# Rounded pairs for the experts' down product: 19 pieces of its weights prepared in the input projection, 45 in the output projection

## The reference

```
proj = x @ w_in                       # 1024 -> 1536: u, v, xs
y_a  = gelu(u) * spatial_gate(layer_norm(gelu(v)))          # 4 heads, 128x128 causal
y_b  = s5_state_space(xs)             # 32 groups, 64 complex states, then a GLU
x    = layer_norm(ALPHA * x + concat(y_a, y_b) @ w_out)
# grouped top-2 of 16 experts, D_FF = 256
h    = silu(x @ w_gate[e]) * (x @ w_up[e])
out += comb[:, e] * (h @ w_down[e])   # w_down[e]: 256 x 1024
x    = layer_norm(ALPHA * x + out)
```

## Time and profile before

| | |
|---|---|
| median of 3 runs | 1351.86 us (1350.22 to 1351.9) |
| the profiled execution | 1347.4 us, span 1345.8 us from first to last instruction |
| busy share of the span | PE 90%, DVE 66%, POOL 35%, ACT 34% |
| DMA | 222.87 MB, 166 GB/s over the span |
| mean granted TensorE clock | 0.957 of 2.4 GHz |

### The profile page before, as it was taken

One profiled execution on the slowest core, in us unless ns is written; L12 is line 12 of the kernel. 1 busy time (PEld: TensorE's weight loads), 2 busy tenths in 40 slices (PEclk: granted clock), 3 DMA queues, 4 the chain that ended last, 5 costly groups with the idle time before them and its releaser, 6 DMA issues. The chain is left out here.

```text
span 1345.8 us, 22978 instructions
## 1 busy us (share of the span) xinstructions
PE 1209.0 (90%) x6813; PEld 969.9 (72%) x6814; DVE 892.6 (66%) x1980; ACT 462.7 (34%) x696; POOL 475.1 (35%) x552
## 2 busy tenths in 40 slices
PE   7999999799978878999999689999999999999910
PEld 6997999778867745888888576777677677677600
DVE  3452776458877655466667677777777777777585
ACT  4120110100003343222221235555565565555433
POOL 3107850210010004322221144454455455445267
PEclk9999999899989998999999699999999999999965
DMA  8555352564154232433332557787887777645484
GB/s 247 184 204 157 102 173 57 137 247 188 64 144 149 90 132 70 156 110 107 127 107 112 207 184 232 211 261 210 241 226 213 214 214 206 141 94 103 117 313 171
DMA packets 112877, 222.87 MB, mean 166 GB/s; under 512 B 51305, under 2 KB 68281, under 8 KB 103569
## 3 DMA queue, kind: packets, MB, share of 16 engines
q1 hardware_dynamic: 96368, 164.86, 36.4%
q0 software_dynamic: 15408, 55.12, 17.6%
q10 hardware_dynamic: 1040, 2.10, 0.4%
HBM read 144.34 MB, written 77.58 MB: 165 GB/s over the span
## 5 line engine op out<-in xcount | busy, mean ns | idle before, releaser
L2055 DVE TENSOR_TENSOR wgu<-w_raw,wgu (+1 forms) x192 | 226.1, 1220 | 52.5 <-ACT wgu L2142 52.4
L2249 PE MATMUL p_gu<-wgu,xg_high 128*128 x768 | 251.4, 408 | 4.5 <-DVE xg_low L2048 4.5
L2142 ACT CAST wgu<-w_raw (+1 forms) x192 | 187.1, 1050 | 18.9 <-SPq L1863 16.3
L2249 PEld LDWEIGHTS p_gu<-wgu,xg_high 128*128 128x128 f32 x768 | 143.2, 188 | 58.0 <-issue 30.9
L2272 PE MATMUL p_d<-wd,ht 128*128 x384 | 174.9, 598 | 1.8 <-DVE ht L2069 1.0
L2249 PE MATMUL p_gu<-wgu,xg_low 128*128 x384 | 150.3, 391 | 0.0
L2272 PEld LDWEIGHTS p_d<-wd,ht 128*128 128x128 f32 x384 | 69.0, 189 | 71.3 <-issue 71.2
L1721 PE MATMUL p_out<-w_out_high,mixt_high 128*128 128x512 f32 x256 | 101.4, 396 | 0.0
L1721 PE MATMUL p_out<-w_out_high,mixt_low 128*128 128x512 f32 x256 | 99.9, 390 | 0.0
L1721 PE MATMUL p_out<-w_out_low,mixt_high 128*128 128x512 f32 x256 | 99.7, 389 | 0.0
L1934 POOL TENSOR_TENSOR spare_e<-nothing 128x1 f32<-128x1 f32 x48 | 9.2, 192 | 227.7 <-DVE yo L2075 227.7
(11 more groups left out here) (441 smaller groups left out, 2727.2 us busy)
## 6 DMA issues: line engine op xcount, KB each, us to landing
w_raw<-in_w_gate SPq DMA_DIRECT2D x16, 1024.0 KB, 4.7
w_raw<-in_w_up SPq DMA_DIRECT2D x16, 1024.0 KB, 7.7
wd<-in_w_down SPq DMA_DIRECT2D x16, 1024.0 KB, 4.8
acc_rows<-ax SPq DMA_DIRECT2D x18, 512.0 KB, 5.6
xin<-in_x_prompt SPq DMA_DIRECT2D x16, 512.0 KB, 6.2
sq<-sq_mats SPq DMA_DIRECT2D x16, 512.0 KB
z<-in_x_prompt SPq DMA_DIRECT2D x16, 512.0 KB, 4.1
x_rows<-x SPq DMA_DIRECT2D x16, 512.0 KB, 4.8
```

The lines of the kernel that those rows point to most:

```text
L2055: low = tt(wgu[:, slot, 1, at], raw[:, slot, at], wgu[:, slot, 0, at].bitcast(F32), ALU.subtract)
L2142: nc.scalar.copy(wgu[:, slot, 0, at], raw[:, slot, at]).then_inc(hi_set, 1)
L2249: mm = t.matmul(pg[b][:, :, :], x[:, b, k, :], w[h][:, k], start=(k == 0 and x is xh and h == 0), stop=(k == KD - 1 and x is xl))
```

## The change

The down product becomes a product of rounded pairs too. The high and low halves of `w_down` are made once for each expert, ahead of the expert stage, written to DRAM (`wd_dram`) and read back there. The weights are cut into 64 pieces of 128 partitions x 512 columns (2 KB runs), four to an expert. A piece takes one load (SP), one rounding copy (ACT), one subtraction (DVE) and two stores (SP).

- 19 pieces in the input projection, steps 6 to 23 and 26, at most one in a step: load at step n, ACT at n + 1, DVE at n + 2, stores at n + 3. Their room is that of `ya` tiles not yet written (y4 to y7) and of two of the four `xin` slots (x2, x3); x rows go through the other two slots from row tile 4 on, and their loads move behind the stores of odd steps.
- 45 pieces in the output projection, in steps p = 2 to 15: 2, 1, 3, 2, 3, 4, 3, 4, 4, 4, 4, 4, 4, 3. They lie in tiles of `ya` (the piece, then its low half) and `yb` (the high half) that are used up. SP, ACT and DVE have these steps unrolled.
- `ya` and `yb` are laid out by tile of 128 tokens ([P, 16, 4, 128] in place of [P, 4, 2048]).
- Expert stage: two arrays of down weights are loaded in place of one; `ht` gets a high half (ACT) and a low half (DVE); ACT and DVE take the quarters of the weights in another order, with a semaphore for each quarter; the two transposes of the hidden rows stand in the middle of `gate_up`; the rows of ln2 are loaded at the end of the stage.

```diff
@@ input projection
+            SLOTS = {"x2": 30, "x3": 30, "y4": 16, "y5": 20, "y6": 24, "y7": 28}
+            LIFE = 4
+            for n in range(6, 27):
+                free = [s for s in SLOTS if busy.get(s, 0) <= n and n + LIFE <= SLOTS[s]]
+                free.sort(key=lambda s: SLOTS[s])
+                for s in free[:1]:
+                    if len(UNITS) < 19:
+                        UNITS.append((n, s))
+                        busy[s] = n + LIFE
...
+                def rows_in(c):
+                    before = c - 4 if c < 6 else c - 2
+                    sp.wait_ge(turned[before % 4], before // 4 + 1)
+                    sp.dma_start(xin[:, c % 2, :], x_rows[c * P:(c + 1) * P, :]).then_inc(load_x[c % 2], 16)
+
+                def units(n):
+                    for j, s, m in units_at(n - 3):
+                        sp.wait_ge(wd_low, j + 1)
+                        for h in range(2):
+                            sp.dma_start(wd_dram[h][j // 4, :, j % 4 * SUP:(j % 4 + 1) * SUP],
+                                         wd_part(s, 1 - h, True).bitcast(F32)).then_inc(wd_st[s], 16)
+                    for j, s, m in units_at(n):
+                        if m:
+                            sp.wait_ge(wd_st[s], m * 32)
+                        elif s[0] == "x":
+                            sp.wait_ge(turned[int(s[1])], 1)
+                        sp.dma_start(wd_part(s, 0, False), wd_src[j // 4, :, j % 4]).then_inc(wd_ld[s], 16)
...
+                        if i and f % 2 and 2 * i + 4 + f // 2 < CH:
+                            rows_in(2 * i + 4 + f // 2)
+                        units(n)
@@ ACT, u_tile(i, f)
+                    for j, s, m in units_at(i * FT + f - 1):
+                        act.wait_ge(wd_ld[s], m * 16 + 16)
+                        nc.scalar.copy(wd_part(s, 1, True), wd_part(s, 0, False)).then_inc(wd_high, 1)
@@ DVE, xs_tile(i, f)
+                    for j, s, m in units_at(i * FT + f - 2):
+                        dve.wait_ge(wd_high, j + 1)
+                        v.tensor_tensor(wd_part(s, 0, True), wd_part(s, 0, False), wd_part(s, 1, True).bitcast(F32),
+                                        ALU.subtract).then_inc(wd_low, 1)
@@ output projection, SP
+                def units_in(p):
+                    sp.wait_ge(mix_low, p * 2 + 2)
+                    if landed(p - 2, 2, 32):
+                        sp.wait_ge(wd_st[p % 2], landed(p - 2, 2, 32))
+                    for u, t in STEPS_D[p]:
+                        sp.dma_start(ya_u[:, t], wd_src[u // 4, :, u % 4]).then_inc(wd_ld[p % 2], 16)
+
+                def units_out(p):
+                    sp.wait_ge(wd_low, landed(p, 1, 1))
+                    for u, t in STEPS_D[p]:
+                        for h in range(2):
+                            sp.dma_start(wd_dram[h][u // 4, :, u % 4 * SUP:(u % 4 + 1) * SUP],
+                                         (yb_r, ya_r)[h][:, t].bitcast(F32)).then_inc(wd_st[p % 2], 16)
+
+                for p in range(2, CH + 1):
+                    sp.wait_ge(x1_set, p + 1)
+                    if p in STEPS_D:
+                        units_in(p)
+                    if p < CH - 1:
+                        rows_in(p, p % 2)
                     stores(p, p % 2)
+                    if p - 1 in STEPS_D:
+                        units_out(p - 1)
@@ output projection, ACT
+                def units(p):
+                    act.wait_ge(wd_ld[p % 2], landed(p, 2, 16))
+                    for u, t in STEPS_D[p]:
+                        nc.scalar.copy(yb_r[:, t], ya_u[:, t]).then_inc(wd_high, 1)
+
+                for p in range(2, CH):
+                    if p + 2 <= CH:
+                        high(p + 2, p % 2)
                     tile(p, p % 2, p // 2)
                     score(p - 1)
+                    units(p)
@@ output projection, DVE
+                def units(p):
+                    dve.wait_ge(wd_high, landed(p, 1, 1))
+                    for u, t in STEPS_D[p]:
+                        v.tensor_tensor(ya_r[:, t], ya_u[:, t], yb_r[:, t].bitcast(F32), ALU.subtract).then_inc(wd_low, 1)
...
                         norm(i * 2 + b, b, False, i)
                         turn(i * 2 + b - 1, (b + 1) % 2)
+                        units(i * 2 + b - 1)
                     select(i * 2 - 4, 2, i * 2 - 1)
...
                 turn(CH - 1, 1)
+                units(CH - 1)
                 norm(CH, 0, False, CH // 2)
@@ experts, SP
                 def down(e):
-                    sp.dma_start(wd[:, 1 - e % 2, :], a["w_down"][0, expert(e)].rearrange("(p k) f -> p (k f)", p=P)).then_inc(wd_in[e % 2], 16)
+                    for h in range(2):
+                        sp.dma_start(wd[h][:, 1 - e % 2, :].bitcast(F32), wd_dram[h][expert(e)]).then_inc(wd_in[e % 2], 16)
@@ experts, DVE, step
                 def tail(i, b, first):
-                    dve.wait_ge(h_turned, i + 1)
-                    v.tensor_copy(ht[:, b], pt_h[:, :, :]).then_inc(ht_set, 1)
+                    dve.wait_ge(ht_high, i + 1)
+                    tt(ht[1][:, b], pt_h[:, :, :], ht[0][:, b].bitcast(F32), ALU.subtract).then_inc(ht_set, 1)
...
+                        prep(i, slot, range(1))
                     if begun:
                         result(i - 2, b, begun == 1)
                     if not last:
-                        prep(i, slot, range(3))
+                        prep(i, slot, range(1, 3))
                     if begun or b:
                         tail(i - 1, 1 - b, False)
+                    if not last:
+                        prep(i, slot, range(3, 4))
                     hidden(i, b, not begun)
                     if not last:
                         turn(i + 1, 1 - b)
-                        prep(i, slot, range(3, 4))
@@ experts, ACT, step
                     if not last:
                         slot, ready = regs(i)
+                        prep(i, not begun and b == 0, slot, ready)
                     if begun:
                         result(i - 2, b, begun == 1)
                     if not last:
-                        prep(i, not begun and b == 0, slot, ready)
+                        for c in range(1, 3):
+                            quarter(i, slot, c)
+                    if begun or b:
+                        hidden_high(i - 1, 1 - b, not begun or begun == 1 and b == 0)
+                    if not last:
+                        quarter(i, slot, 3)
@@ experts, PE
-                    w = wd[:, slot, :].rearrange("p (k n) -> p k n", k=2)
+                    w = [wd[h][:, slot, :].rearrange("p (k n) -> p k n", k=2) for h in range(2)]
                     for m in range(2):
                         for k in range(2):
-                            mm = t.matmul(pd[m][:, :], ht[:, b, k, :], w[:, k, m * SUP:(m + 1) * SUP], start=(k == 0), stop=(k == 1))
+                            for x, h in PARTS:
+                                mm = t.matmul(pd[m][:, :], ht[x][:, b, k, :], w[h][:, k, m * SUP:(m + 1) * SUP],
+                                              start=(k == 0 and x + h == 0), stop=(k == 1 and x == 1))
...
                     for k in range(KD):
+                        if k == KD // 2 and between:
+                            between()
```

More of the change, by code:

```diff
@@ L136, in hybrid_step @@
         x1_dram = dram("x1_rows", [SEQ + NS, D])
+        wd_dram = [dram(f"w_down_{n}", [E, P, 4 * SUP]) for n in ("high", "low")]
+        wd_src = a["w_down"][0].rearrange("e (p k) (h f) -> e p (k h) f", p=P, h=2)
+        NUNITS = 4 * E
         acc_dram = dram("acc_rows", [SEQ + NS + 2 * P, D])
@@ L396, in _ @@
                 act.wait_ge(w_v_in, 16)
+                for s in ("x2", "x3"):
+                    act.wait_ge(wd_st[s], uses(s) * 32)
                 for k in range(KD):
@@ L1432, in hybrid_step, with landed @@
             x1_stored = [phase_sem(f"x1_stored{i}") for i in range(2)]
+            wd_ld, wd_st = ([phase_sem(f"d_wd_{k}{i}") for i in range(2)] for k in ("in", "stored"))
+            wd_high, wd_low = sems("d_wd_high d_wd_low")
+            STEPS_D, used, left = {}, {}, NUNITS - AUNITS
+            for p in range(2, CH):
+                free = [t for t in range(p) if used.get(t, 0) <= p - 2][:min(3 + (p in (7, 9, 10, 11, 12, 13, 14)), left)]
+                STEPS_D[p] = [(NUNITS - left + k, t) for k, t in enumerate(free)]
+                left -= len(free)
+                used.update((t, p) for t in free)
+            assert left == 0, left
+            def landed(p, of, each):
+                return sum(len(u) for q, u in STEPS_D.items() if q <= p and (q - p) % of == 0) * each
             ax1_stored = [phase_sem(f"ax1_stored{i}") for i in range(2)]
@@ L1691, in _ @@
                     turn(1 + b, 1 - b, b == 0)
+                units(2)
                 dve.wait_ge(sel_set, 7)
                 dve.wait_ge(rb_in, 16)
-                with dve.Fori(2, CH // 2 - 1) as i:
-                    ch.enter(i - 2, 8 + 32)
+                for i in range(2, CH // 2 - 1):
```

(15 more changed lines are left out.)

114 lines of the change are left out of this document (70 added, 44 removed).

## The result

The changed kernel took 1359.26 us (median of 6 runs, 1356.13 to 1361.83) against 1351.19 us of the kernel before on the same chip: ratio 1.0062, 95% interval [1.0044, 1.008]. It is slower by 0.6%. The forecast was 1329 us and "faster" with 0.90, so both sign and time failed.

A forecast was written before the change was run, and what follows sets the result against it. The expert stage was taken to go at PE's pace. Down product -35.5, last tile +0.5, expert DMA +2, output projection +4 and +4.3, input projection +2 gave -22.7: 1351.9 to 1329 us, range 1317 to 1346.

The forecast's parts named there:

- Preparing the pieces, output projection: Output projection: making 45 pieces in 14 steps costs +4 us in the steps and +4.3 at the stage's end.
- SP and DMA term: Output projection: loads queued behind landing stores need 13.8 us against a 13.6 us step; +4 us, bounds 0 and 25.
- Both signs that the prediction named for being wrong: Whole kernel: PE's total does not fall by 35 us, or the two projections together grow by over 20.
- rival C: Output projection: all 14 steps go at the pace of stores landed, then loads; slower, 1373 us, threshold 1352; chance 0.07.
- The end of the stage, +4.3: Output projection's end: the last step's pieces stand before the last norm with nothing covering them; +4.3 us, bounds 2 and 6.
- ACT's and DVE's work: Output projection: copies and subtractions mostly fit DVE's slack; 0 to 1 us a pair of four-piece steps, 4 such pairs.
- Input projection, +2, bounds 0 and 11.6: Input projection: 19 pieces, one a step, mostly covered, ACT 1 to 2 us late in places; +2 us, bounds 0 and 11.6.
- The down product, -35.5: Expert stage: 12 rounded products at p_gu's 0.228 us save 0.74 us a tile over 48 tiles, -35.5 us.
- DMA in the experts, +2: Expert stage: 14 more loads of 1.05 MB fit by 3% but land later; +2 us, bounds 0 and 15.
- Rival A: Expert stage: it slips off PE as gate_up waits for xg_low; +14 us at 0.3 us a tile, 1343 us; chance 0.12.
- B: Expert stage: the DMA engines fill up, with 92% busy in two-tile experts; 1344 us; chance 0.10.
- D (1321): Both projections: preparation is hidden but for the output projection's tail; -30.7 us, 1321 us; chance 0.16.

The follow-up runs named there:

- run 11: Changed kernel with the output projection's piece loads and stores left out, ACT's and DVE's work kept on a resident row, unrounded down weights read: 1333.34 us.
- run 9: Changed kernel with 40 output-projection pieces, the last step's behind the last norm, tiles reused after three steps, unrounded down weights read: 1339.5 us.
- run 10: Same kernel as run 9, but tiles reused after two steps, so SP waits for the stores of step p - 2: 1348.09 us.
- run 7: Changed kernel with three output-projection orders changed and high halves not stored, experts reading them from w_down itself: 1334.99 us, ratio 0.9888 to the kernel before.
- run 2: Changed kernel storing only 128 of 512 columns of each output-projection half, experts reading unrounded down weights: 1343.99 us.
- run 5: Changed kernel with only the last step's three pieces moved behind the last norm, on ACT and DVE: 1352.03 us.
- run 4: Changed kernel with no pieces prepared in either projection, experts reading unrounded down weights: 1321.64 us, ratio 0.98 to the kernel before.
- run 8: Changed kernel with one step more between a piece's load and ACT's rounding in the input projection, steps 4 to 24: 1346.38 us.
- run 3: Changed kernel without the 45 output-projection pieces, the 19 input-projection pieces kept, experts reading unrounded down weights: 1326.33 us.
- run 1: Changed kernel with ACT rounding the output projection's pieces one step later: 1356.61 us, ratio 1.0056 to the kernel before.
- run 12: Changed kernel with the order of run 5, the single store of run 7 and the lead of run 8: 1331.83 us, ratio 0.9856 to the kernel before.

## Why the prediction was wrong

**The step that failed** is "Preparing the pieces, output projection", its SP and DMA term: +4, bounds 0 and 25. With the transfers that also struck the end of the stage, it measured 25.8 us (run 11 against the kernel after: 18.0 in the loop, 7.8 at the end). The mechanism was named, and its pair of numbers was "even", 13.8 against 13.6; I then took a value near the lower bound. Both signs that the prediction named for being wrong came: the two projections grew by 38.5 us together, and PE's busy time fell by 15.1 us and not by 35 (27 less in the experts, 11 more in the output projection, 2 more in the input projection). Three errors lay in the 13.8:

- *The rate.* 400 GB/s was read in two microseconds. It does occur in this traffic (417 and 397, above), but only for 4 us behind the loads; over 50 us it is 341 at full share, and 4.72 MB take 13.8 us and not 11.8. That alone is PE's step of 13.6. The Trainium skill, "DMA: Bandwidth & Descriptors", section Where 436 GB/s comes from, gives about 358 GB/s for a core's HBM side. Over a step the trace stays below it; inside a step it was exceeded again (417), so the page's figure is no ceiling here, but as a mean it would have served better than mine.
- *The turn.* I allowed 2 us of latency between the last store's bytes and the next load's. It measured 17.2 - 13.8 = 3.4 us a step (the share of 0.80). Behind it stands SP: it needs 8.0 us to issue 4 loads, z, x, the accumulator and 6 stores (661.62 to 669.6), and 8.7 to 11.2 with 8 stores, a cost that was in no term, and only then can the last landing begin to be waited for (8.2 us). Making that wait one step older gave 6 us (runs 9 and 10); one store fewer, which cuts issue, bytes and wait at once, gave 12 (run 7).
- *"Only six steps have four."* By the forecast's own list seven have four, and steps 7 to 15 have four or three without a gap, and what is late is not caught up. "It is even" was the sign to put rival C near the forecast and not at 0.07. C's threshold was close: it asked for +26.7 us in 14 steps, and the transfers cost 25.8. Its rate was not: it wanted less than 290 GB/s at full share (304 with the mean of 4.1 MB a step that 45 pieces make, where the prediction has 3.9), where 341 with a fifth of the time idle was enough.

**The end of the stage, +4.3, was right in mechanism and for its own work:** the last interval is longer by 4.2 in run 11 and by 4.3 in run 2. In the kernel after it is 12.0, since the same loads are late there. Behind the norm, the pieces cost 7.9 less (run 5).

**ACT's and DVE's work: right.** 0 to 1 us a pair of steps had been foreseen, 1.3 in ten steps came (run 11).

**Input projection, +2, bounds 0 and 11.6: too small.** It was 6.4 us by the table and 7.2 against run 4. The forecast saw ACT "1 to 2 us late" with a step in hand; ACT waited 23.7 us in seven waits of up to 5.8, since these loads take 5.2 and 4.5 us to land there (medians by tile), where the DMA engines are at a share of up to 1.01, and not the 3.6 us of the earlier trace rows. Run 8 shows it was the lead, not the work.

**The down product, -35.5: right in kind, and the saving a fifth smaller.** In the chain it is 3.46 - 2.80 = 0.66 us a tile, 31.7 in 48 tiles: 12 products go at 0.233 us each and not at the 0.228 of p_gu. From the first p_d of a tile to that of the next, the mean of 47 fell from 10.05 to 9.48 us, 26.8 in all. The other 0.09 us a tile matches idle time of PE, none in 350 us before and 3.3 in 340 after; the profile names nothing that PE waits for there. (The prediction calls the down product's multiplications a third of p_gu's. They are half, 4 logical products of 512 columns to 8; the sum makes no use of it.) The first p_d also comes later behind the first p_gu, 18.6 us against 15.5. Its window in the kernel after and, for the same tile, in run 7:

```profile
829.00:845.00 16.00, 12.63 (x44) 10.15 (x45) 10.81 (x12) 9.65 (x12) 2.94 (x5) 0.79 0.55 225
```

```profile
806.00:822.00 16.00, 11.53 (x58) 9.49 (x57) 11.87 (x14) 11.67 (x15) 4.40 (x8) 1.00 0.60 230
```

With the same products, and about as many bytes, the clock was 0.79 in the one and 1.00 in the other. The first p_d comes at 15.5 us in runs 3, 7 and 9, at 17.0 in runs 1, 2, 4, 8 and 11, and at 18.5 to 18.7 in the others. So 3 us of what the experts' -24.3 lacks against the chain's 31.7, and of the miss in run 12, stand in this tile's slower clock. What decides the clock there is open.

**DMA in the experts, +2: little showed, and nothing that is surely DMA's in PE's chain.** In the tightest 50 us:

```profile
900.00:950.00 50.00, 48.60 (x235) 40.18 (x234) 36.89 (x46) 32.66 (x48) 26.22 (x30) 1.00 0.97 308
```

At a share of 0.97, with loads an expert ahead, PE is idle 1.4 of 50 us, with no releaser named; whether the full DMA engines lie behind that, and behind the 0.09 us a tile above, is not shown. ACT waited for weights to land 3.5 us in two waits from 850 us on. Rival A did not come: xg_low is what p_gu waits for during 4.5 us in both kernels. Of B no more than these few us can have come. D (1321) would have needed the preparation hidden; run 4, with none at all, is 1321.64.

**The sum in measured terms:** 6.4 - 1.1 + 32.1 + 0 - 24.3 = +13.1 of span. What stays open: why the loads' part of a step runs at 294 GB/s at full share and the rest at 367, what PE waits for in its short gaps in the expert stage, and the 2.6 us by which run 8 is shorter than a stage without pieces.

## What to carry to other kernels

When a store must land before the next load may start, add issue time, transfer and landing, and take the rate from a window as long as the traffic will be; where that sum only equals the step, count on losing it, since a queue that is late stays late. Judge such a chain by a run with the transfers left out before mending orders: here the longest waits of DVE (50 us for a root) went away without any gain, while one transfer fewer in each piece was worth 12 us. Put side work behind a stage's last norm: ahead of it, its place alone cost 8 us here (run 5).

## What the runs showed of the hardware

- At full share the DMA engines moved between 237 and about 410 GB/s inside one step of the output projection, 341 as the mean of 50 us, 308/1.01 = 305 in the input projection and 308/0.97 = 318 with the experts' loads. A short window says nothing of the mean.
- A store of 256 KB kept SP 0.45 to 1.45 us in issuing it and landed after 6.5 to 7.2 us (median), against 3.6 for such a transfer in the kernel before.
- Float32 words that were never rounded can stand as the high operand of the pair products, with the low half still made against the rounded value (runs 7 and 12). What PE itself does with their last bits is not shown.
- The granted clock over the output projection was 0.96 before, 0.95 with no transfers (run 11) and 0.90 after. At 676.6 us PE began again after 3.1 us of standing still; the clock went to 0.50, and up to 686.8 its products of 512 columns came 0.43 us apart in place of 0.23. In the experts' first tile, low stretches took 3.1 us; what they took in the output projection, where SP's chain set the pace, is not shown.
